# Retention scores by 32-row slices in pairs of heads, and the mixer's norms by token quarters

## The reference, cut to what matters

```python
def conformer_conv(u, conv_w, conv_b, ln_w, ln_b):
    a, g = jnp.split(u, 2, axis=-1)
    h = a * jax.nn.sigmoid(g)
    h = ...depthwise convolution, 31 taps, 256 channels... + conv_b
    return jax.nn.silu(layer_norm(h, ln_w, ln_b))

def retention step (4 heads, dk 32, dv 64):
        inner = jnp.einsum('bhqd,bhkd->bhqk', qc, kc) * decay_in
        y = jnp.einsum('bhqk,bhkv->bhqv', inner, vc) + ...

def retention_out(y, g, gn_w):            # mean and variance over the 64 of a head
    yn = ((y - mu) * lax.rsqrt(var + NORM_EPS)).reshape(b, n_tok, h * dv).astype(g.dtype)
    return jax.nn.silu(g) * (yn * gn_w)

q  = rms_norm(cq, q_norm_w) @ w_uq        # cq: 256 wide
kv = rms_norm(ckv, kv_norm_w) @ w_ukv     # ckv: 128 wide
```

## Time and profile before

| | |
|---|---|
| median of 3 runs | 2279.25 us (2275.8 to 2280.16) |
| profiled execution | 2269.91 us, span 2268.1 us |
| TensorE (matmul) busy | 2125.4 us, 94% |
| VectorE busy | 930.6 us, 41% |
| ScalarE busy | 512.7 us, 23% |
| chain that ended last | PE 67%, DMA 23%, DVE 6%, issue 2%, ACT 1% |
| mean granted clock of TensorE | 0.978 |

### The profile page before, as it was taken

How to read it: one execution, slowest core, us unless ns; L and a number is a source line. 1 busy time by engine, 2 the same in 40 slices (tenths; PEclk the granted TensorE clock), 3 DMA queues, 4 the chain that set the end, 5 groups by cost and what they waited for, 6 DMA issues and landing times.

```text
span 2268.1 us, 37581 instructions
## 1 busy us (share of the span) xinstructions
PE 2125.4 (94%) x13292; PEld 1288.7 (57%) x13292; DVE 930.6 (41%) x1862; ACT 512.7 (23%) x1073; POOL 678.2 (30%) x811
## 2 busy tenths in 40 slices
PE   6998989999999999999998998899999998899997
PEld 2474345455666666666666663354456665566663
DVE  2394676413722222222226776662453232222235
ACT  4313154303111111111114612452300000000003
POOL 0000000000356566565641000000045555545540
PEclk9999989999999999999999999999999999999999
DMA  9611000264499999999998221000269999999996
GB/s 372 241 54 63 0 0 1 111 260 186 158 374 419 419 418 419 418 419 419 420 380 341 80 79 37 1 1 22 109 272 417 417 416 415 417 416 415 414 396 272
DMA packets 88905, 594.75 MB, mean 262 GB/s; under 512 B 25318, under 2 KB 25582, under 8 KB 44016
## 3 DMA queue, kind: packets, MB, share of 16 engines
q1 hardware_dynamic: 52704, 525.25, 56.4%
q0 software_dynamic: 34672, 63.07, 7.4%
q10 hardware_dynamic: 1440, 5.24, 0.6%
HBM read 573.46 MB, written 60.56 MB: 280 GB/s over the span
## 4 chain that ended last, share of the span: by engine, by line
PE 67%; DMA 23%; DVE 6%; issue 2%; ACT 1%; SPq 1%; POOL 0%; POOLq 0%; DVEq 0%; ACTq 0%
PE psum L1135 19%; DMA arena<-in_experts 15%; PE psum L748 12%; PE psum L1160 10%; PE psum L987 6%; PE psum L920 3%; DMA arena<-y 3%; PE psum L948 2%; DMA arena<-hrows,IX 2%; DMA arena<-in_mod_w 2%; PE psum L832 2%; PE psum L965 2%; PE psum L858 2%; PE psum L762 2%; DVE arena L1664 1%
## 5 line engine op out<-in xcount | busy, mean ns | idle before, releaser
L1135 PE MATMUL psum<-arena 128*64 128x256 f32 x6144 | 710.6, 383 | 31.6 <-DMA arena<-in_experts 27.8
L1135 PEld LDWEIGHTS psum<-arena 128*64 128x64 f32 x6144 | 520.9, 138 | 159.2 <-issue 39.3
L2257 POOL DMA_INDIRECT arena<-hrows,IX x384 | 394.1, 1026 | 223.9 <-POOL IX L2249 156.0
L1160 PE MATMUL psum<-arena 128*64 128x512 f32 x1536 | 370.8, 597 | 11.9 <-DMA arena<-in_experts 10.4
L748 PE MATMUL psum<-arena 128*128 128x512 f32 (+1 forms) x880 | 330.9, 532 | 9.8 <-DVE arena L1841 7.1
L2265 POOL DMA_INDIRECT y<-arena,IX x192 | 197.4, 1028 | 275.6 <-DVE arena L2086 124.5
L748 PEld LDWEIGHTS psum<-arena 128*128 128x128 f32 x880 | 168.9, 195 | 162.6 <-issue 139.6
L1534 ACT ACTIVATE arena<-psum 128x128 f32<-128x128 f32 x192 | 53.3, 278 | 850.0 <-PE psum L1135 850.0
L2086 DVE STREAM_TRANSPOSE arena<-arena 128x512 f32<-128x512 f32 x192 | 135.6, 706 | 207.1 <-DMA arena<-hrows,IX 205.7
L1160 PEld LDWEIGHTS psum<-arena 128*64 128x64 f32 x1536 | 131.4, 137 | 131.1 <-issue 115.7
L2093 DVE TENSOR_TENSOR arena<-psum,arena 128x128 f32<-128x128 f32 x192 | 55.2, 288 | 348.5 <-ACT arena L1534 347.9
(11 more groups left out here) (269 smaller groups left out, 1936.3 us busy)
## 6 DMA issues: line engine op xcount, KB each, us to landing
arena<-in_experts SPq DMA_DIRECT2D x128, 2048.0 KB, 21.5
arena<-in_experts SPq DMA_DIRECT2D x128, 1024.0 KB, 23.9
arena<-in_mod_w SPq DMA_DIRECT2D x48, 1024.0 KB, 7.7
arena<-y SPq DMA_DIRECT2D x20, 1536.0 KB, 17.2
arena<-in_wblk SPq DMA_DIRECT2D x22, 1024.0 KB, 4.9
arena<-in_shared SPq DMA_DIRECT2D x2, 3072.0 KB, 12.9
arena<-hrows,IX POOLq DMA_INDIRECT x384, 11.1
hrows<-arena ACTq DMA_DIRECT2D x10, 512.0 KB, 2.6
```

The source lines that it names most:

```text
L1135: last = mm(psum[j * ROWS:(j + 1) * ROWS, (0, 1, 5)[u], 0:2 * P], HT[:, u, k, :], w[:, k * 512 + j * 256:k * 512 + (j + 1) * 256], start=k ...
L1160: last = mm(psum[q * ROWS:(q + 1) * ROWS, (3, 4, 6)[u], :], AT[:, u, j * ROWS:(j + 1) * ROWS], w[:, 4096 + j * D + q * 512:4096 + j * D + ...
L2257: g.indirect_dma_start(GR[:, r, h * 256:(h + 1) * 256], None, rows, offsets(IX[:, s, h:h + 1]), bounds_check=4 * T * P - 1, oob_is_err=Fal ...
```

## The change

Five things, in both layers:

1. The scores of a head are a product over its own 32 partitions of RK and RQ, without QM; the two scores of a pair stand one behind the other and go to different PSUM banks. QM and the mask multiplies are gone.
2. The norms cv, cqn, ckvn and gv go by token quarters: `token_sums` with the matching constant, narrow root, narrow reciprocal (`token_roots`), `spread_roots`. For gv a new constant `headrow` spreads two heads to 64 partitions each. RSB now has 16 places of 128 columns.
3. The squares, sums and roots of cv, cqn and ckvn move into the last projection group, behind ckv 0, ckv 1 and kr 0; cm comes ahead of the rotations of q and k.
4. The folds kf, the rotation of kr and the spreads of the latents are done one behind the values of each pair (`beside_pair`). VectorE takes the narrow reciprocals at units 4, 6, 8, ..., the rotation of kr at unit 5, and the scalings, which now read the spread from PSUM, at units 7, 9, 11, ...
5. Behind the loop the gate and gn_w are multiplied in first, and the spread of the roots last (L1830 of the new file); the spreads stand between the query projections.

```diff
                 if z == ("cq", 1, sq[-1]):
-                    steps += [("rot", "q"), ("rot", "k")] + [("cm", s) for s in sq]
-                if z[0] == "ckv" and z[1] in sq:
-                    steps.append(("cv", z[1]))
+                    steps += [("cm", s) for s in sq] + [("rot", "q"), ("rot", "k")]
+                if z == ("ckv", 0):
+                    steps += [("cv", s) for s in sq]
+                if z == ("ckv", 1):
+                    steps += [("cqn", s) for s in sq]
+                if z == ("kr", 0):
+                    steps += [("ckvn", s) for s in (0, 1)]
...
         for i in range(4):
-            j += [(("qn", i, 0), "A")]
-            j += [(("gv",) + halves[i], "A")] if i < len(halves) else []
-        j += [(("qr", r, 0), "A") for r in range(2)] + [(("rot2", r), "D") for r in range(2)]
+            self.queries += [("qn", i, 0)] + [("gv",) + x for x in halves[i:i + 1]] + [("bc", "gv") + x for x in halves[i - 2:i - 1] if i >= 2]
+        for r in range(2):
+            self.queries += [("qr", r, 0)] + [("bc", "gv") + x for x in halves[r + 2:r + 3]]
+        self.queries += [("rot2", r) for r in range(2)]
...
-                pe.wait_ge(sem("q_masked"), HEADS_R * (l + 1))
-
-                def ret_scores(u):
-                    s, h, kt = units[u]
-                    a, n = SEG[s]
-                    if u >= 4:
-                        pe.wait_ge(sem("ret_p"), decays_before(l) + u - 3)
-                    mm(psum[:, u % 4, 0:n], RK[:, kt * P:(kt + 1) * P], QM[:, h, a:a + n],
-                       start=True, stop=True).then_inc(sem("ret_s"), 1)
+
+                def ret_scores(pair):
+
+                    if pair >= 4:
+                        pe.wait_ge(sem("ret_p"), decays_before(l) + pair - 2)
+                    for u in (pair, pair + 1):
+                        s, h, kt = units[u]
+                        a, n = SEG[s]
+                        rows = slice(DK_R * h, DK_R * (h + 1))
+                        mm(psum[:, u % 4, 0:n], RK[rows, kt * P:(kt + 1) * P], RQ[rows, a:a + n],
+                           start=True, stop=True).then_inc(sem("ret_s"), 1)
+
+                def beside_pair(m):
+
+                    if m == 0:
+                        for s in (0, 1):
+                            a, n = SEG[s]
+                            evacuated(pe, l, ("kr", s))
+                            product(("kf", s), ROPE, [(c("fold4"), CAT[:, 7, a:a + n])], n)
+                    elif m == 1:
+                        evacuated(pe, l, ("kf", 0))
+                        product(("rot", "kr"), ROPE, [(c("perm", ROPE)[:, 0:ROPE], CAT[0:ROPE, 7, 0:LAT])], LAT)
+                    elif m - 2 < len(pl.latents):
+                        spread_roots(pl.latents[m - 2])
...
                 for u, (s, h, kt) in enumerate(ret_units(l)):
-                    if u % 4 == 3 and latents:
-                        key, q, chunks = latents.pop(0)
-                        a, n = SEG[q]
-                        r = recip((key, q), n)
-                        for k, w, i in chunks:
-                            last = V.scalar_tensor_tensor(CAT[:, k, a:a + n], CAT[:, k, a:a + n], pr(l, w, i), r, ALU.mult, ALU.mult)
-                        last.then_inc(norm_used, 1)
+                    if u >= 4 and u % 2 == 0 and (u - 4) // 2 < len(pl.latents):
+                        token_roots(pl.latents[(u - 4) // 2])
+                    if u == 5:
+                        evacuated(dve, l, ("kf", 0))
+                        rope("kr", CAT[0:ROPE, 7, 0:LAT], TMPK, ROPE)
+                    if u >= 7 and u % 2 == 1 and (u - 7) // 2 < len(pl.latents):
+                        normalised(pl.latents[(u - 7) // 2])
```

More of the change, by code:

```diff
@@ L490, in rooted @@
         def rooted(l, key):
[L493 removed]
+            return 1 + plans[l].norm[key]
         def y_slot(t):
@@ L1306, in _ @@
                         continue
-                    if kind == "cv":
+                    if kind in ("cv", "cqn", "ckvn"):
                         a, n = SEG[st[1]]
-                        evacuated(act, l, ("cm", st[1]))
-                        squares(st, [CAT[:, b, a:a + n] for b in range(2)], n)
-                        root(st, n)
+                        evacuated(act, l, {"cv": ("cm", st[1]), "cqn": ("cq", 1, st[1]), "ckvn": ("ckv", st[1])}[kind])
+                        squares(st, [CAT[:, b, a:a + n] for b in {"cv": (0, 1), "cqn": (4, 5), "ckvn": (6,)}[kind]], n)
+                        root(st)
                         continue
@@ L1370, in _ @@
                     a, n = SEG[s]
-                    evacuated(act, l, ("cq", 1, s))
-                    squares(("cqn", s), [CAT[:, 4 + b, a:a + n] for b in range(2)], n)
-                    root(("cqn", s), n)
-                evacuated(act, l, ("ckv", 1))
-                for s in (0, 1):
-                    a, n = SEG[s]
-                    squares(("ckvn", s), [CAT[:, 6, a:a + n]], n)
-                    root(("ckvn", s), n)
-                for s in pl.sq:
-                    a, n = SEG[s]
-                    act.wait_ge(sem(f"norm_used{l}"), pl.norm[("cv", s)] + 1)
+                    evacuated(act, l, ("bc", "cv", s))
                     for b in range(2):
```

189 lines of the change are left out of this document (90 added, 99 removed).

## The result

The changed kernel takes **2256.98 us** (median of 5, 2255.95 to 2263.85) against 2275.8 us for the kernel before in the same session (median of 5, 2269.59 to 2280.16). The medians are 18.8 us apart, where 15.1 were forecast. The ratio on record, 0.9929 with a 95% interval of 0.9914 to 0.9944, stands for 16.2 us (12.7 to 19.6): faster, clear of the noise. The 2264 us forecast stood on a median of 2279.25; on the session's own median it would have been 2260.7. The profiled execution of the changed kernel has a span of 2255.2 us.

A forecast was written before the change was run, and what follows sets the result against it. TensorE, busy 94% of the span, carries most of the chain, so only starting a layer's attention sooner pays. Terms -4.3 - 2.1 - 5.1 - 4.8 + 0.3 + 0.9 = -15.1 took 2279.25 to 2264 us; range 2253 to 2277.

The forecast's parts named there:

- rival (b): TensorE keeps the full clock ahead of the loops, so the clock charges fall away: 2257 us; chance 0.13.
- The low level: TensorE at 1.2 GHz after sparse stretches: charged 2.3 us ahead of loop 0, 2.8 in it, about 2.0 in loop 1.
- Ahead of the loop: From ckv 0 to the first scores, latent sums and roots moved between products: -4.3 us in layer 0, -4.8 in layer 1.
- The series of hand-overs: Ahead of the loop, latent norms pass serially between ScalarE and TensorE; layer 0 reordered saves 6.6 us before the clock charge.
- Loop, layer 0: Retention loop of layer 0: 45.5 us against 50.4, less 2.8 us lost to the 1.2 GHz clock: -2.1 us.
- The full-clock ring: In the loops, a norm pair runs values, spread, hand-over, scaling, multiply in series: 3.2 to 4.4 us; rotation pair 4.9.
- Loop, layer 1: Retention loop of layer 1: 38.0 us against 39.7 at full clock, plus about 2.0 at a lower clock: +0.3 us.
- Behind the loop, layer 0: From means to attention, the queries' rotation starts at 20.3 us against 22.8 and slow clock after the wait goes: -5.1 us.
- Behind the loop, layer 1: From means to attention, the queries' rotation starts 17.6 us behind the means against 16.6: +0.9 us.
- The slices: In the loops, two 32-row score products overlap and cost 0.96 us instead of 1.91.
- rival (a): In the loops, row slices do not overlap, a pair stays at 2.9 us: 2278 us; chance 0.13.
- Rival (c): TensorE stays at 1.2 GHz through both loops: 2307 us, deciding from about 30 us beyond the 10 counted; chance 0.07.

The follow-up runs named there:

- the run with the rotation first: Changed kernel with the queries' rotation moved ahead of the head norms' spreads and products behind the retention loops: 2261.5 us, ratio 0.9945.
- the last kernel above: Changed kernel with each pair's spread ahead of its values and scores over all 128 rows instead of 32-row slices, masked copies left out: 2259.69 us, ratio 0.9951.

## Why the prediction was right, and where it was off

The measured 2256.98 us lies in the stated range and 1 us below the forecast's own band of 2258 to 2269, in the place of rival (b). Each of the six stages came within 2 us of its term, and the mechanism of each is in the trace. The low level in the loops is the part that held by luck, as told below.

**Ahead of the loop (-4.3, measured -6.1; layer 1 -4.8, measured -5.1).** The series of hand-overs was read rightly: 6.6 us less at full clock. The charge for the low level, +2.3, was mis-sized: it fell behind 217 us, not at 210, and doubled only the last part of kr (1.97 us for 1.07 in layer 1's trace), 0.9 us. Less 6.6, plus 0.9, is -5.7; the other 0.4 I did not follow up.

**Loop, layer 0 (-2.1, measured -0.5).** The full-clock ring was right: the pair with the rotation takes 4.92 us (229.20 to 234.12; forecast 4.9), the last five of the six norm pairs 3.68, 3.61, 3.29, 4.14 and 3.56 (forecast 3.6, 3.7, 3.2, 4.4 and 3.6), a bare pair 2.07 (forecast 1.96). The 64-wide spread, taken at 0.85, takes 1.04 (240.71 to 241.75). The step that failed is the low level's price. I had 2.8 us from one episode. There were two. The loop's start to its second scores took 8.10 us against 4.99 in layer 1 at full clock, +3.1; and the pair at 234.12, behind the rotation's wait, took 5.58 (above the 5 that I had said would break the term) where 4.4 were forecast, +1.2. Together 4.3, 1.5 more than charged, which is nearly the whole miss of 1.6. And that the price was no higher was luck: in the run with the rotation first, the same loop stood some 23 us at the low level in place of 11 and took 53.60 us, 3.2 more than before and not 2.1 less. I had counted on an episode of 5.6 us of work; nothing in my rows bounded it.

**Loop, layer 1 (+0.3, measured -0.3).** 38.0 at full clock plus 2.0 was forecast, 39.39 came. The low level came elsewhere than I thought: not at the start, but behind the 1.82 us wait that ends at 1388.50 (granted clock 0.57 from 1388 to 1392), and cost 1.4. In the other execution of the same loop it cost 3.2 (41.24 us).

**Behind the loop, layer 0 (-5.1, measured -4.4).** The rotation starts on VectorE 20.8 us behind the means (290.81 - 269.99; forecast 20.3), and this half microsecond is most of the 0.7 that the term is off. The wait of TensorE for it is 1.75 us in place of 3.02 and 2.19, and the low level behind it is gone, as forecast: 1.00 where the kernel before had 0.76 in the second half.

**Behind the loop, layer 1 (+0.9, measured -0.2).** The rotation starts 18.05 us behind the means (1434.96 - 1416.91; forecast 17.6). What I left out: the kernel before had a low level here too, 0.89 over 15.8 us, and its last 14 products took 6.27 us where they now take 4.57. From the end of TensorE's wait to the first attention scores it is 6.15 us where it was 7.76. These 1.6 us turn the 1.4 that the rotation starts later into -0.2. I had counted the low level in layer 0 and not in layer 1.

**The slices.** 0.96 us for two was taken, 1.06 came; not at all overlapping would have been 1.91, so rival (a) is out. The Trainium skill, TensorE: Matmul & The Clock Gate, Part 3, gives 3.07 times for four row tiles; the estimate taken from it was 1.24 us for two, and the measurement, 1.06 us or 1.8 times for two, is better than that. The Trainium skill, TensorEngine Tiling (Array Packing), Key Properties, has TensorE drain when the tiling mode changes. The trace agrees, at about 0.1 us: two full-row scores take 1.82 us up to a full-width spread (230.56 to 232.38) and 1.91 us up to 64-column values (256.21 to 258.12) in the last kernel above, and a spread costs the loop 1.09 us behind slices and 0.99 us behind full rows. I had charged 0.17 by this rule; the forecast without it was nearer.

**Rival (b)**, full clock kept, gave 2257, which is the number that came, but not for its reason: both loops had their low level. Of the 7 us between 2264 and 2257, 3.5 are a session whose kernel before was faster, 1.5 are the stages, and some 2 are the difference between profiles and medians, which no stage shows. **Rival (c)**, slower at 2307, was to decide from 30 us of low level beyond the 10 counted (its own terms give 2308). The changed kernel had some 11 us in loop 0 and 4 in loop 1, in the other execution 23 and 10, so it stood nearer than I thought. Slices alone fall into it. What ends it, the idle products suggest, is work over all rows between the pairs, and the change puts such work there, the spreads, which I had counted only as a cost of 1.1 us each. That it is the spreads that save the change is argued from those runs, not shown by taking them away. The slices need the other half: with full rows the change gave 11.5 us, the slices alone -19.6, both 18.8.

**What I didn't see.** The order within a pair. I priced a norm pair as a ring in series, values, spread, scaling, multiply, and took its order as given. The ring's waits were in my own sum; moving the spread into them gives 17 us, and with them goes the low level that made the price of the loop a matter of luck.

## What to carry to other kernels

Put independent work of TensorE where it waits, ahead of the instruction that waits and not behind it: here one moved line was worth 17 us, nearly as much as the whole change. A change that leaves the array emptier (row slices, narrow products) must be judged with the granted clock of its stretch: check that some full-array work remains between the slices, and price the waits not only by their length but by the low level that can follow them, whose length a single profile doesn't tell. Where a sum of forecast terms holds a ring in series, ask first whether its links have to be in series.

## What the runs showed of the hardware that I had not expected

- TensorE can be busy without a gap and stay at 1.2 GHz: 28.2 us on end (253.76 to 281.95) in a loop of 59.9 us at 0.50, with 32-row scores and 64-column values only.
- An idle product can shorten a kernel: 16 idle 128x512 products between the pairs took 27.9 us off it, the same ones over 32 rows 20.6 us.
- A wait of 1.82 us in a loop of slices, values and spreads was followed by 3.4 to 14.8 us at the low level in the eight loops read here, of four kernels with the same order in them. In the kernel before, with full-row scores, a wait of 2.31 us was followed by some 4 us of it in layer 0 (two scores at 235.47 took 3.05 us) and by none in layer 1 (two scores at 1400.19 took 1.98).
- Two 32-row slices take 1.06 us against 1.91 for two full products; a third one beside them is free where it has rows of its own (1.06 us for the three, 257.32 to 258.38), and comes on top where it shares its rows with one of them.
